# RG-LRU gate products as 64 by 64 tiles, in a ring of four PSUM banks, around the first key product

## What is computed

```python
def _rglru(xb, gb, h0, conv_buf, conv_w, conv_b, w_a, b_a, w_x, b_x, lam):
    ...                                             # xc: causal convolution of width 4
    xh = xcf.reshape(bsz, s, LRU_HEADS, LRU_HEAD_DIM)          # 8 heads of 64
    r = sigmoid(einsum("bshi,hij->bshj", xh, w_a) + b_a).reshape(bsz, s, D_LRU)
    ig = sigmoid(einsum("bshi,hij->bshj", xh, w_x) + b_x).reshape(bsz, s, D_LRU)
    log_a = -LRU_C * r * softplus(-lam)
    a = exp(log_a)
    b = sqrt(-expm1(2.0 * log_a)) * (ig * xcf)
    b = b.at[:, 0].add(a[:, 0] * h0)
    _, h = associative_scan(_real_diag_combine, (a, b), axis=1)
    y = h * gelu(gb)
```

## Time and profile before

| what | us |
|---|---|
| median of 3 runs | 1131.98 (1129.73 to 1132.42) |
| span of the profiled execution | 1131.9 |
| the stage of the change, from the first gate product to the first GLU product | 247.62 to 323.10 |
| TensorE busy | 1080.0 of 1131.9 |

### The profile page before, as it was taken

The page is one execution under the profiler, slowest core; times in us unless marked ns, Lnnn a source line. Parts: engine busy times, 40 slices in busy tenths (PEclk is TensorE's granted clock), DMA queues, the critical chain, the costliest instruction groups (busy, mean ns, idle before and its releaser), DMA issues.

```text
span 1131.9 us, 15627 instructions
## 1 busy us (share of the span) xinstructions
PE 1080.0 (95%) x6183; PEld 617.9 (55%) x6183; DVE 697.6 (62%) x1352; ACT 277.9 (25%) x570; POOL 186.8 (16%) x221
## 2 busy tenths in 40 slices
PE   6999999999999999999999999999999999999992
PEld 4666766678765444688866645545733333333330
DVE  4576499927866755743266767766553555555555
ACT  5201321246652111110033311110301223222232
POOL 5000010101000000000000000000122355574465
PEclk9999999999999999999999999999999999999996
DMA  9109450178382301400044542025889999999952
GB/s 298 46 1 211 42 42 1 41 216 284 118 322 97 85 0 33 190 1 1 1 186 169 199 153 94 20 75 186 288 268 391 414 411 413 413 416 413 409 211 86
DMA packets 75244, 204.97 MB, mean 181 GB/s; under 512 B 25480, under 2 KB 34336, under 8 KB 66816
## 3 DMA queue, kind: packets, MB, share of 16 engines
q1 hardware_dynamic: 54336, 168.82, 42.6%
q0 software_dynamic: 20704, 35.09, 9.2%
q10 hardware_dynamic: 128, 0.03, 0.0%
HBM read 195.23 MB, written 52.18 MB: 219 GB/s over the span
## 4 chain that ended last, share of the span: by engine, by line
PE 80%; DMA 7%; DVE 6%; issue 4%; POOL 1%; ACT 1%; ACTq 0%; POOLq 0%; another core or an unknown queue 0%; DVEq 0%
PE bank L803 16%; PE bank L966 9%; PE bank L1338 9%; PE bank L1031 9%; PE bank L1161 6%; PE bank L775 5%; PE bank L1356 4%; DMA work_firsts<-arena,slots_in 3%; PE bank L925 3%; PE bank L1063 2%; PE bank L1128 2%; DMA arena<-work_rows,slots_in 2%; DMA arena<-work_firsts,ptmp 2%; PE bank L892 2%; PE bank L1326 1%
## 5 line engine op out<-in xcount | busy, mean ns | idle before, releaser
L803 PE MATMUL bank<-arena 128*128 128x360 f32 (+1 forms) x576 | 179.6, 472 | 1.0 <-DVE arena L1770 0.9
L1338 PE MATMUL bank<-arena 128*32 128x512 f32 x1536 | 171.7, 599 | 0.9 <-DVE arena L2500 0.9
L803 PEld LDWEIGHTS bank<-arena 128*128 128x128 f32 x576 | 109.5, 192 | 65.8 <-issue 3.2
L2089 DVE TENSOR_TENSOR arena<-arena,bank 128x512 f32<-128x512 f32 (+3 forms) x56 | 68.4, 1221 | 66.1 <-PE bank L1031 37.4
L1338 PEld LDWEIGHTS bank<-arena 128*32 128x32 f32 x1536 | 47.7, 110 | 106.5 <-issue 105.3
L966 PE MATMUL bank<-arena 128*128 128x272 f32 x448 | 103.0, 392 | 0.0
L1161 PE MATMUL bank<-arena 128*128 128x512 f32 x224 | 100.6, 598 | 1.0 <-DVE arena L2254 1.0
L1031 PE MATMUL bank<-arena 128*128 128x512 f32 x224 | 97.7, 593 | 0.0
L966 PEld LDWEIGHTS bank<-arena 128*128 128x128 f32 x448 | 85.0, 190 | 17.4
L1440 ACT ACTIVATE arena<-bank 128x272 f32<-128x272 f32 (+5 forms) x92 | 41.1, 448 | 192.9 <-PE bank L803 130.2
L1356 PE MATMUL bank<-arena 128*32 128x512 f32 x768 | 87.4, 592 | 0.1
(11 more groups left out here) (447 smaller groups left out, 1470.1 us busy)
## 6 DMA issues: line engine op xcount, KB each, us to landing
arena<-in_w_gate SPq DMA_DIRECT2D x32, 1024.0 KB
arena<-in_w_up SPq DMA_DIRECT2D x32, 1024.0 KB
arena<-in_w_down SPq DMA_DIRECT2D x32, 1024.0 KB
arena<-in_ck SPq DMA_DIRECT2D x8, 1024.0 KB, 7.5
arena<-in_cv SPq DMA_DIRECT2D x8, 1024.0 KB, 5.5
arena<-in_w_in SPq DMA_DIRECT2D x3, 2048.0 KB, 13.9
work_firsts<-in_x SPq DMA_DIRECT2D x1, 4352.0 KB
arena<-in_x SPq DMA_DIRECT2D x8, 512.0 KB, 5.9
```

What stands on the lines that cost most here:

```text
L803: last = nc.tensor.matmul(b[:, 0:w], win[slot][:, k, m * P:m * P + P], ht[:, k, c0:c0 + w], start=k == 0, stop=k == KD - 1)
L1338: last = nc.tensor.matmul(bank[2 + j % 2][t0:t0 + QT, :].rearrange("p (h n) -> p h n", h=2), xgt[j % 2][:, k, t0:t0 + QT], gu[e % GUB][:, ...
L2089: V.tensor_tensor(out, out, bank[banks(n)][:, :].unsqueeze(1).to_broadcast([P, width, 512]), ADD).then_inc(sem["md_free"], 1)
```

## The change

The gate weights become 64 by 64 tiles without the zero blocks (`wab` is 128 by 2 by 4 by 64). For each chunk, four products run, one for each gate a and head h. The head h is on rows 64h to 64h + 63. Gate 0's head h is written to partitions 64h of its bank, gate 1's head h to the other half of its own bank (`out = 64 * ((h + a) % 2)`), so that the four products of a chunk use the four quarters of the array. Both fills of a chunk come from the ring `TAY` of four banks. Chunks 0 and 1 come first in a round, chunk 2 stands in the middle of the first memory product (after 4 of its 8 contraction steps).

ScalarE drains a chunk with three activations in place of two: gate 0 in one over 128 partitions, gate 1 in two over 64 partitions each, which also swap the halves back. They are Tanh with scale 0.5 and half the bias; the sigmoid is half of that tanh plus one half. The later Tanh and Exp take the half in their scale and bias, VectorE's first operation takes `ti + 1` in place of `ti`, and one that multiplied by 2 is a plain product. `table(ACT.Exp)` stands where `table(ACT.Sigmoid)` stood. The zero fill of the weights on GpSimd and its semaphore go; VectorE makes the halved biases in one small operation more. Counts are moved to fit the rings.

```diff
-            nc.gpsimd.memset(wab[:, :, :, :], 0.0).then_inc(sem["wab_zero"], 1)
...
-            sp.wait_ge(sem["wab_zero"], 1)
             for a, w in enumerate(("w_a", "w_x")):
                 for h in range(2):
-                    sp.dma_start(wab[64 * h:64 * h + 64, a, :, 64 * h:64 * h + 64], I[w][h]).then_inc(sem["gate_w_in"], 16)
+                    sp.dma_start(wab[64 * h:64 * h + 64, a, :, :], I[w][h]).then_inc(sem["gate_w_in"], 16)
...
-            def memory(q):
+            def memory(q, m, b=None, k0=0, k1=KD):
...
-            def gates(c):
+            def gates(c, ci):
 
-                if c == 0:
+                c0, w = CHUNKS[ci]
+                if c == 0 and ci == 0:
                     pe.wait_ge(sem["gate_w_in"], 64)
-                    pe.wait_ge(sem["xc_ok"], CT)
-                for a in range(2):
-                    for c0, w in CHUNKS:
-                        b = claim(MA, ma, "ma_free")
-                        nc.tensor.matmul(b[:, 0:w], wab[:, a, c, :], xc[:, c, c0:c0 + w], start=True, stop=True).then_inc(sem["ma_full"], 1)
+                if ci == 0:
+                    pe.wait_ge(sem["xc_ok"], c + 1)
+                fills = [claim(TAY, ta, "ta_free") for a in range(2)]
+                for a, b in enumerate(fills):
+                    for h in range(2):
+                        rows_, out = slice(64 * h, 64 * h + 64), 64 * ((h + a) % 2)
+                        last = nc.tensor.matmul(b[out:out + 64, 0:w], wab[rows_, a, c, :], xc[rows_, c, c0:c0 + w], start=True, stop=True)
+                    last.then_inc(sem["ta_full"], 1)
...
             for c in range(CT):
-                gates(c)
+                gates(c, 0)
+                gates(c, 1)
                 if c in (1, 2):
                     key_t(c - 1)
-                memory(2 * c)
-                memory(2 * c + 1)
+                b = memory(2 * c, 0, None, 0, 4)
+                gates(c, 2)
+                memory(2 * c, 0, b, 4, KD)
+                memory(2 * c, 1)
+                for m in range(MT):
+                    memory(2 * c + 1, m)
...
-                for a, dst in enumerate((tr, ti)):
-                    for c0, w in CHUNKS:
-                        bias = par[:, COL[("lru_b_a", "lru_b_x")[a]] + c:][:, 0:1]
-                        drain(MA, ma, "ma_full", dst[:, c0:c0 + w], w, ACT.Sigmoid, "ma_free", bias=bias)
-                act.wait_ge(sem["ma_free"], ma.n + 1)
-                link(nc.scalar.activation(ts_[:, :], tr[:, :], ACT.Tanh, scale=m4sp[:, c:c + 1]))
-                nc.scalar.activation(tr[:, :], tr[:, :], ACT.Exp, scale=m8sp[:, c:c + 1]).then_inc(sem["te_ok"], 1)
+                drain(TAY, ta, "ta_full", tr[:, c0:c0 + w], lambda bk: bk[:, 0:w], ACT.Tanh, "ta_free", scale=0.5, bias=gate_b[:, c:c + 1])
+                n = ta.next()
+                act.wait_ge(sem["ta_full"], n + 1)
+                for h in range(2):
+                    rows_, src = slice(64 * h, 64 * h + 64), 64 * (1 - h)
+                    last = nc.scalar.activation(ti[rows_, c0:c0 + w], bank[TAY[n % 4]][src:src + 64, 0:w], ACT.Tanh, scale=0.5, bias=gate_b[rows_, 4 + c:5 + c])
+                last.then_inc(sem["ta_free"], 1)
+
+            def lru_exps(c):
+                tr, ti, ts_ = lru_w[c % 2]
+                act.wait_ge(sem["ta_free"], ta.n + 1)
+                link(nc.scalar.activation(ts_[:, :], tr[:, :], ACT.Tanh, scale=m2sp[:, c:c + 1], bias=m2sp[:, c:c + 1]))
+                nc.scalar.activation(tr[:, :], tr[:, :], ACT.Exp, scale=m4sp[:, c:c + 1], bias=m4sp[:, c:c + 1]).then_inc(sem["te_ok"], 1)
...
             for c in range(CT):
-                lru_gates(c)
+                for ci in range(3):
+                    gate_rows(c, ci)
+                lru_exps(c)
                 drain_kv(2 * c)
...
-                link(V.tensor_tensor(xcc, xcc, ti[:, :], MUL), V.tensor_scalar(tr[:, :], tr[:, :], 0.5, 0.5, MUL, ADD))
+                link(V.scalar_tensor_tensor(xcc, ti[:, :], 1.0, xcc, ADD, MUL), V.tensor_scalar(tr[:, :], tr[:, :], 0.5, 0.5, MUL, ADD))
...
-                link(V.scalar_tensor_tensor(ts_[:, :], ts_[:, :], 2.0, tr[:, :], MUL, MUL))
+                link(V.tensor_tensor(ts_[:, :], ts_[:, :], tr[:, :], MUL))
```

More of the change, by code:

```diff
@@ L56 @@
 tp_full tp_free ta_full ta_free ma_full ma_free md_full md_free act_own dve_own pool_own ident_ok std_ok xn_ok
-dt_ok ang_ok trig_ok scal_ok gnat_ok h_ok klag_ok wab_zero t_zero small_ok par_ok par_full spx_ok xc_ok
+dt_ok ang_ok trig_ok scal_ok gnat_ok h_ok klag_ok t_zero small_ok par_ok par_full spx_ok xc_ok
 te_ok sqrt_arg sq_ok ylru_ok end_ok hs_ok spv_full spo_ok ydc_ok yg_ok lru_ends kv_out small_out ut_in
@@ L86, in hybrid_layer @@
         ssq = sb("ssq", [P, 12])
-        m4sp, m8sp, spt = sb("m4sp", [P, 4]), sb("m8sp", [P, 4]), sb("spt", [P, 24])
+        spt = sb("spt", [P, 24])
         zero1 = sb("zero1", [P, 2])
@@ L147, in hybrid_layer @@
         sig = [reg(38912 + 408 * s, 408) for s in range(2)]
-        wab = reg(R_TMP + 2336, 2, CT, P)
+        wab = reg(R_TMP + 2336, 2, CT, 64)
         parin = q16[:, 0, :]
@@ L161, in hybrid_layer @@
         TP, TA, MA, MD = (0, 1), (6, 7), (2, 3), (4, 5)
+        gate_b, m2sp, m4sp = par[:, 104:112], par[:, 112:116], par[:, 116:120]
         stin = [q16[:, 0, :], q16[:, 1, :]]
@@ L180, in kv_fills @@
         def kv_fills(q):
-            return 58 + 10 * (q // 2) + 2 * (q % 2) + MT
-        MA_U, MA_X1, MA_S, MA_X, MA_G, MA_KV = 12, 20, 36, 40, 52, 92
+            return MA_G + MT * (q + 1)
+        MA_U, MA_X1, MA_S, MA_X, MA_G, MA_KV = 12, 20, 36, 40, 52, 68
         MA_Y = MA_KV + 12
@@ L192, in hybrid_layer @@
         Y_TA0 = 8
+        TA_LRU = Y_TA0 + GRP
+        TA_ATT = TA_LRU + 2 * len(CHUNKS) * CT
         R_E2 = R_XL + NT * D
@@ L767, in norm_t @@
                 tile_t(xst[n % XR], ROWS[n])
-            def memory(q):
-                pe.wait_ge(sem[f"wkv_in{q % 3}"], 16 * (q // 3 + 1))
-                for m in range(MT):
+            def memory(q, m, b=None, k0=0, k1=KD):
+                if k0 == 0:
+                    pe.wait_ge(sem[f"wkv_in{q % 3}"], 16 * (q // 3 + 1))
                     b = claim(MA, ma, "ma_free")
-                    for k in range(KD):
-                        last = nc.tensor.matmul(b[:, 0:KQ], mt_[:, k, m * P:m * P + P], wkv[q % 3][:, k, :], start=k == 0, stop=k == KD - 1)
+                for k in range(k0, k1):
+                    last = nc.tensor.matmul(b[:, 0:KQ], mt_[:, k, m * P:m * P + P], wkv[q % 3][:, k, :], start=k == 0, stop=k == KD - 1)
+                if k1 == KD:
                     last.then_inc(sem["ma_full"], 1)
+                return b
             def key_t(h):
@@ L1136, in obank @@
                 elif OB[n] in TA:
-                    pe.wait_ge(sem["ta_free"], Y_TA0 + GRP + 3 * NB - 1 + (OB[n] == 7))
+                    pe.wait_ge(sem["ta_free"], TA_ATT + 3 * NB - 1 + (OB[n] == 7))
                 else:
@@ L1439, in drain @@
                 act.wait_ge(sem[full], n + 1)
-                nc.scalar.activation(out, bank[ring[n % 2]][0:out.shape[0], 0:w] if isinstance(w, int) else w(bank[ring[n % 2]]), func, **kw).then_inc(sem[free], 1)
+                nc.scalar.activation(out, bank[ring[n % len(ring)]][0:out.shape[0], 0:w] if isinstance(w, int) else w(bank[ring[n % len(ring)]]), func, **kw).then_inc(sem[free], 1)
             def drain_u(ci, m):
@@ L1512, in table, with gate_rows @@
                 link(nc.scalar.activation(warm[:, :], zero1[:, 1:2], func))
-            def lru_gates(c):
+            def gate_rows(c, ci):
                 tr, ti, ts_ = lru_w[c % 2]
-                if c >= 2:
+                c0, w = CHUNKS[ci]
+                if c >= 2 and ci == 0:
                     act.wait_ge(sem["ylru_ok"], c - 1)
-                for a, dst in enumerate((tr, ti)):
-                    for c0, w in CHUNKS:
-                        bias = par[:, COL[("lru_b_a", "lru_b_x")[a]] + c:][:, 0:1]
-                        drain(MA, ma, "ma_full", dst[:, c0:c0 + w], w, ACT.Sigmoid, "ma_free", bias=bias)
-                act.wait_ge(sem["ma_free"], ma.n + 1)
-                link(nc.scalar.activation(ts_[:, :], tr[:, :], ACT.Tanh, scale=m4sp[:, c:c + 1]))
-                nc.scalar.activation(tr[:, :], tr[:, :], ACT.Exp, scale=m8sp[:, c:c + 1]).then_inc(sem["te_ok"], 1)
+                drain(TAY, ta, "ta_full", tr[:, c0:c0 + w], lambda bk: bk[:, 0:w], ACT.Tanh, "ta_free", scale=0.5, bias=gate_b[:, c:c + 1])
[10 more added lines that the diff above has]
+                nc.scalar.activation(tr[:, :], tr[:, :], ACT.Exp, scale=m4sp[:, c:c + 1], bias=m4sp[:, c:c + 1]).then_inc(sem["te_ok"], 1)
             def lru_root(c):
@@ L1540, in _ @@
                 if g == GRP - 8:
-                    table(ACT.Sigmoid)
+                    table(ACT.Exp)
             act.wait_ge(sem["spx_ok"], 2)
             for c in range(CT):
-                lru_gates(c)
+                for ci in range(3):
+                    gate_rows(c, ci)
```

(7 more changed lines are left out.)

## The result

The changed kernel takes 1124.69 us (median of 4 runs, 1123.86 to 1126.99) beside 1132.2 us of the kernel before on the same chip. The ratio is 0.9928, 95% interval 0.9907 to 0.995: faster by 7.5 us (5.7 to 10.5 by the interval), where 7.6 were forecast. The profiled execution has a span of 1122.8 us, 9.1 less than before.

What follows compares the result with a forecast made beforehand. TensorE, busy 1080.0 of 1131.9 us, bounds the kernel; gates of 1.83 + 0.80 = 2.63 us a round make 10.5 for 18.15, 7.6 us less: 1131.98 - 7.6 = 1124.4 us, range 1121 to 1131.

Steps and rivals of the forecast that it cites:

- Four at once: TensorE gates: a chunk's four small products overlap in one stream, 1.83 us a round; forecast 1124.4 us, chance 0.71.
- changes of tile: TensorE gates: each switch between full and smaller tiles costs 0.20 us, four a round, 0.80 us.
- two at once: Rival, TensorE gates: two heads writing one bank take turns, two streams a chunk, 4.46 us a round; 1131.6 us, chance 0.12.
- One bank, two halves of the rows: TensorE gate fills: products of different rows write one bank without taking turns, since their partitions differ; one stream a chunk.
- The table load: ScalarE, in front of the Exp: one load a round less, 1.28 us, if Exp and Tanh share a table.
- ScalarE late: Rival, ScalarE's gate and key drains: slack used up, 1127.2 us, or with a load more 1130.4; chance 0.12.
- VectorE: VectorE's rounds and tail: 14.1 us stays under the new 16.4 us round; last bank freed 0.3 us before the fifth fill.
- Whole to the end: Behind the stage: every trigger hangs on TensorE's progress, so 7.6 us should reach the end whole.
- The chances: Outcome odds for the whole kernel: faster by more than 0.3% 0.79, within it 0.16, slower 0.05.
- the slack of 0.2 to 0.6 us: ScalarE's first key drain: ends 0.6 us before TensorE claims the bank, 0.2 us where no transposes stand between.

Runs made afterwards that it cites:

- Zero blocks: Changed kernel with 128 by 128 gate weights and their zero blocks again, everything else kept; 1128.2 us, 0.9963 of the kernel before.
- two quarters: Changed kernel with gate 1 not crossed, so a chunk's products use two quarters of the array; 1132.52 us, 1.0 of the kernel before.
- a bank for each half of the rows: Changed kernel with a chunk's fills split by head, not by gate (LRU gates get each other's values); 1122.68 us, 0.9926 of the kernel before.
- The swap: Changed kernel with ScalarE draining a round's third memory fill in front of the Sqrt, not behind it; 1123.9 us, 0.9929 of the kernel before.
- the second time: The changed kernel, unaltered, profiled and timed once more; 1125.8 us, 0.9941 of the kernel before.
- sigmoids again: Changed kernel with sigmoids in place of the half tangents, tiles, banks and order kept; 1128.73 us, 0.9977 of the kernel before.
- tiles alone: Kernel before with the 64 by 64 tiles only, keeping its ring of two banks, order and sigmoids; 1155.74 us, 1.0216 of the kernel before.
- half tangents alone: Kernel before with only the half-scale Tanh, halved biases, Exp table and matching VectorE operations; 1132.93 us, 1.0007 of the kernel before.
- filling the waits: Kernel before with only the 64 by 64 tiles, plus unread products in TensorE's waits; 1144.66 us, 1.0116 of the kernel before.
- chunk 2 not inside the key product: Changed kernel with chunk 2 right behind chunks 0 and 1; 1128.65 us, 0.9969 of the kernel before.

## Why the prediction was right

- **Four at once** held. The gates stream 1.83 us a round with 0.80 at the changes of tile, and round 0 is the 16.44 us of the sum. Zero blocks (3.9 us of 4.1 expected) and two quarters (6.3 of 7.3) price it from both sides. The rival *two at once* is what the kernel with two quarters does, and it ends where the rival said, at 1132.5 for 1131.6.
- **One bank, two halves of the rows.** The Trainium skill (TensorEngine Tiling (Array Packing), Restrictions and Gotchas) says that different row tiles cannot access one PSUM bank at the same time. By that rule a chunk would have taken two streams. This trace doesn't agree: a chunk of 360 columns takes 0.77 us with its change of tile, and the same with a bank for each half of the rows. The partitions differ here; both on the same partitions was not tried.
- **The table load** went, by the trace. The Trainium skill (ScalarE: Activation LUTs, Table sets: the hidden batching unit) has exp and tanh in one set, and the trace agrees: two loads a round for three.
- **ScalarE late** came true in small. I had 0.2 us left in round 3 and lost 0.17. ScalarE began that round's gates 1.36 us into it (300.02 less 298.66), as late as reckoned, and its first key drain at 9.12, where 8.5 and the lateness of 0.36 make 8.86: the nine gate drains took 5.23 us for 5.1, and Tanh and Exp, with a bias tile 1.29 us each for 1.20, the rest. In rounds 1 and 2 there is a wait that the prediction didn't name: the transposes need the last key drain of the round before, which 4.47 us of gates had covered and 1.5 don't. The swap gave back 0.24 and 0.09 us there and 0.07 in round 3, 0.40 together.
- **VectorE** ended its rounds and the tail as worked out (drained at 325.13, bank free in time for the fifth fill).
- **Whole to the end** held as far as it can be seen: 7.61 us in the stage, 7.5 in the medians, 6.5 in those of the second time.
- **That 7.61 meets 7.6** is luck. The prediction's pieces make 75.1 us of the stage before (4 x 13.81 + 18.15 + 2 x 0.87), and it took 75.48: round 3's gates were 4.64 us, not 4.47, and the memory products of rounds 0 and 3 took 0.08 more each. The same pieces make 67.5 us of the new stage, and it took 67.87, by the waits above. Two misses of nearly 0.4 us cancel.
- **The chances** don't quite follow from their own words: with half of *ScalarE late* on each side they would be 0.77 and 0.18, not 0.79 and 0.16.
- **What the load carries** the prediction gave in its rival *ScalarE late*: 6 us back, had the kernel had a load a round more than now. With just as many as before (sigmoids again) 4.4 us went. So the forecast hung on this load more than its bound says, and the slack of 0.2 to 0.6 us was as thin as written.
- The expectation that failed is that of the tiles alone: the waiting was reckoned at 9 us and the clock left out.

## What to carry to other kernels

Small tiles that use all four quarters of TensorE's array are worth their streams only if the drains can follow: price ring, place and tiles together, since tiles alone made this kernel 23.5 us slower and all three 7.5 faster. When the leading engine's round gets shorter, reckon the round of the engines beside it anew, from one release to the next; an edit there that was worth nothing (half tangents alone) may carry half of the gain. And where an edit makes TensorE wait several times in a row, look at the granted clock of that stage too: here two waits of 1.9 us in each round came with stretches at 1.2 GHz, and filling the waits gave 10.4 us back.

## What the hardware showed that I had not expected

- With waits of 1.86 to 1.97 us, two in each round's gates, the granted clock in that stage was 0.84 on average (stretches at 1.2 GHz among stretches at 2.4), and products that filled them kept it at 1.00. A single wait of 1.3 us a round (chunk 2 not inside the key product) left it at 1.00.
- An activation over 1088 columns with a bias tile took 1.29 us for 1.20 without. With sigmoids again, where the scale comes from the same tile and there is no bias, it was 1.20.
- A change between full and quarter tiles costs 0.20 us, as much as between full and half; without changes (zero blocks) the neighbours' streams show no such gap.
